# TensorE's idle products removed from a two-block transformer kernel on one core

## Time and profile before

| | |
|---|---|
| median of three runs | 2423.07 us |
| the profiled execution | 2424.09 us, its span 2422.3 us |
| busy in the span: TensorE products | 2374.6 us (98%) |
| TensorE weight loads | 2012.1 us (83%) |
| VectorE | 1622.1 us (67%) |
| ScalarE | 1115.2 us (46%) |
| GpSimd | 461.2 us (19%) |
| mean granted TensorE clock | 0.995 |
| DMA | 264.29 MB, mean 109 GB/s |

### The profile page before, as it was taken

One profiled execution on the slowest core, in us unless ns is written; L12 is line 12 of the kernel. 1 busy time (PEld: TensorE's weight loads), 2 busy tenths in 40 slices (PEclk: granted clock), 3 DMA queues, 4 the chain that ended last, 5 costly groups with the idle time before them and its releaser, 6 DMA issues.

```text
span 2422.3 us, 38419 instructions
## 1 busy us (share of the span) xinstructions
PE 2374.6 (98%) x16018; PEld 2012.1 (83%) x16018; DVE 1622.1 (67%) x2296; ACT 1115.2 (46%) x1671; POOL 461.2 (19%) x183
## 2 busy tenths in 40 slices
PE   8998989999999999999999999999999999999999
PEld 7747875798989888889898989999887778888887
DVE  6578867896867765679675697666616636666514
ACT  6663544362525445545353554332425435555533
POOL 1312203100000102410000002333134333111234
PEclk9999998999999999999999999999999999999999
DMA  7222453335354343224332323222222322121121
GB/s 298 87 92 66 79 126 139 115 112 185 109 195 158 129 148 114 97 95 149 116 113 94 114 101 122 70 75 83 79 87 89 108 89 103 70 70 70 62 89 67
DMA packets 94413, 264.29 MB, mean 109 GB/s; under 512 B 55201, under 2 KB 55841, under 8 KB 69281
## 3 DMA queue, kind: packets, MB, share of 16 engines
q1 hardware_dynamic: 91936, 253.46, 30.3%
q10 hardware_dynamic: 2304, 8.39, 1.0%
HBM read 256.05 MB, written 5.78 MB: 108 GB/s over the span
## 4 chain that ended last, share of the span: by engine, by line
PE 83%; DVE 8%; issue 3%; DMA 3%; ACT 2%; SPq 0%; DVEq 0%; ACTq 0%; POOL 0%; POOLq 0%
PE bank L357 15%; PE bank L359 15%; PE bank L358 14%; PE bank L2608 6%; PE bank L2610 6%; PE bank L2611 6%; PE bank L290 2%; PE bank L288 2%; PE bank L289 2%; PE bank L4773 1%; DMA ring<-in_stream 1%; PE bank L270 1%; DMA ada_slot<-in_first 1%; PE bank L266 1%; PE bank L267 1%
## 5 line engine op out<-in xcount | busy, mean ns | idle before, releaser
L388 POOL TENSOR_TENSOR ring_low<-ring,w_high 128x2048 fp32r<-128x2048 f32 (+1 forms) x79 | 355.1, 4496 | 1614.3 <-ACT w_high L378 1614.3
L378 ACT ACTIVATE w_high<-ring 128x2048 fp32r<-128x2048 f32 (+1 forms) x128 | 234.7, 1839 | 221.9 <-PE bank L359 212.2
L357 PE MATMUL bank<-h_high,w_high 128*128 128x512 f32 (+1 forms) x480 | 192.3, 401 | 0.0
L359 PE MATMUL bank<-h_high,ring_low 128*128 128x512 f32 (+1 forms) x480 | 190.3, 396 | 0.0
L358 PE MATMUL bank<-h_low,w_high 128*128 128x512 f32 (+1 forms) x480 | 189.1, 394 | 0.0
L357 PE MATMUL bank<-z_high,w_high 128*128 128x512 f32 x380 | 151.3, 398 | 0.1
L359 PE MATMUL bank<-z_high,ring_low 128*128 128x512 f32 x380 | 150.4, 396 | 0.0
L358 PE MATMUL bank<-z_low,w_high 128*128 128x512 f32 x380 | 149.6, 394 | 0.0
L2611 PE MATMUL bank<-h_high,ring_low 128*128 128x256 f32 x528 | 147.2, 279 | 0.0
L359 PE MATMUL bank<-hidden_high,ring_low 128*128 128x512 f32 x352 | 139.5, 396 | 0.0
L357 PE MATMUL bank<-hidden_high,w_high 128*128 128x512 f32 x352 | 139.5, 396 | 0.0
(11 more groups left out here) (594 smaller groups left out, 6802.0 us busy)
## 6 DMA issues: line engine op xcount, KB each, us to landing
ring<-in_stream SPq DMA_DIRECT2D x186, 1024.0 KB, 4.8
ada_slot<-in_ada_next SPq DMA_DIRECT2D x40, 512.0 KB, 4.4
ada_slot<-in_gains SPq DMA_DIRECT2D x17, 512.0 KB, 4.3
ada_slot<-in_first SPq DMA_DIRECT2D x16, 512.0 KB, 4.3
scale_weights<-in_first SPq DMA_DIRECT2D x4, 1024.0 KB, 23.4
inverse<-scratch_inverse SPq DMA_DIRECT2D x32, 128.0 KB, 3.3
x_res<-in_x SPq DMA_DIRECT2D x2, 1024.0 KB, 8.6
w_first<-in_first SPq DMA_DIRECT2D x2, 1024.0 KB, 16.3
```

The source lines that it names most:

```text
L357: pe.matmul(out, w_high[:, k, cols], x_high, start=start, stop=False)
L359: return pe.matmul(out, w_low[:, k, cols], x_high, start=False, stop=stop)
L378: act.activation(self.high_buf[:, b % 2, 0:cols], self.c.ring[:, b % SLOTS, 0:cols], ACT.Copy)\
L388: pool.tensor_tensor(self.c.ring_low[:, b % SLOTS, 0:cols], self.c.ring[:, b % SLOTS, 0:cols], self.high_buf[:, b % 2, 0:cols].bitcast(F32 ...
```

## The change

All calls of `keep_warm` are taken out, and the function with them: 79 products, 158 instructions. No wait, no buffer and no other instruction is changed.

```
@@ Tail.tensor (three borders)
             pe.matmul(c.bank[4][:, j:j + 1], self.acc[:, tok(j)], c.ones[:, 0:1], start=(j == 0), stop=False)
-        c.keep_warm(pe, 1)
         pe.wait_ge(self.squared.sem, self.squared.of(KD - 1))
...
         mm.then_inc(self.mean.sem, 1)
-        c.keep_warm(pe, 2)
         pe.wait_ge(self.inverse.sem, self.inverse.of(0))
...
         mm.then_inc(self.spread.sem, 1)
-        c.keep_warm(pe, 8)
@@ first stage, tensor
         pe.wait_ge(squared.sem, squared.of(0))
-        chip.keep_warm(pe, 16)
         pe.wait_ge(total_of.sem, total_of.of(KD - 2))
...
         mm.then_inc(mean.sem, 1)
-        chip.keep_warm(pe, 4)
         pe.wait_ge(inverse.sem, inverse.of(0))
...
         shift_block(0)
-        chip.keep_warm(pe, 6)
         shift_block(1)
@@ rwkv_output, tensor
         mm.then_inc(var_mm.sem, 1)
-        chip.keep_warm(pe, 12, 0)
...
         for n in range(4):
             spread_tile(n)
-        chip.keep_warm(pe, 8, 0)
```

More of the change, by code:

```diff
@@ L197, in take_groups @@
         return u
-    def keep_warm(self, pe, n, bank=7):
-        for _ in range(n):
-            pe.matmul(self.bank[bank][:, 0:P], self.ident[:, :], self.ones[:, :], start=True, stop=True)
     def slot(self, b, kt):
```

## The result

Median of five runs 2436.45 us (2431.78 to 2440.89), against 2422.66 us (2420.98 to 2424.65) of the kernel before, measured beside it: ratio 1.0054, 95% interval [1.0037, 1.0070]. The changed kernel is slower by 13.1 us in the means (13.8 in the medians); the forecast was 6.4. The profiled execution took 2436.45 us, its span 2434.6 us, mean granted clock 0.987 in place of 0.995.

The account below looks back on a forecast made before the run. TensorE, busy 98% of the span, was taken to set the time. Start +2.1, group norm +2.1 and borders +2.2 gave +6.4 us: median 2423.1 to 2429.5, range 2427.0 to 2432.5, wider 2425.0 to 2435.0.

Parts of the forecast that it names:

- the term of the start: Start: products meet the low clock and L942 ends later; +2.1 us left after slack, bounds +0.7 and +3.9.
- The term of the borders: Three borders: a clock fall at half the visits, 1.5 us each; +2.2 us, bounds -0.2 and +9.2.
- The clock as the cause: All five places: without idle products TensorE's clock is low, 1.2 in place of 2.4 GHz; +6.4 us in all.
- The start's own delay: Start: VectorE's L1208 waits 2.8 us longer for L942; +2.1 us left after slack up to block b_r.
- Spacing and record: Start: product spacing and recorded clock disagree, spacing decides; by record -0.3 us, by spacing +2.1.
- check (4): Between the changed places: equal times for equal work; a difference would make the prediction wrong even with its total right.
- The group norm: Group norm: a certain clock fall slows the output projection, +1.5 us, and the spread, +0.6; sum +2.1, bounds +0.7 and +3.2.
- A fall at every second visit: Three borders: the clock falls at half the visits, 1.5 us a fall; 3 x 0.5 x 1.5 = +2.2 us.
- 263.9 to 267.3: Stretch of the trace before, TensorE busy 1.60 of 3.4 us without a following clock fall; compared with the borders.
- the first rival: Only start and group norm lose the clock, no border falls: 2427.1 us, 0.17% slower; chance 27%.
- Every border falls and comes back late: Rival at the three borders: +9.2 us there, 2436.5 us in all; chance 12%.
- The long low spell: Last rival, recurrence: 13.7 us at half clock cost up to 6.4 us, independent of the change; within the remaining 3%.

Follow-up runs that it names:

- one_column: Kernel before with all 79 idle products kept but each moving one column in place of 128: 2437.10 us, ratio 1.0057.
- no_start_period: Kernel before without the start's 26 idle products, with 64 tiny products ahead of TensorE's first wait: 2430.38 us, ratio 1.0030.
- the tiny products: Kernel before without the start's 26 idle products, with 26 one-column products ahead of TensorE's first wait: 2424.97 us, ratio 1.0013.
- no_gn: Kernel before with only the group norm's idle products (12 and 8) taken out: 2425.19 us, ratio 1.0010.
- no_border: Kernel before with only the borders' idle products (1, 2 and 8, three times) taken out: 2427.69 us, ratio 1.0014.

## Why the prediction was wrong

The direction, the clock's part and the group norm were right; the cost of the start and of the borders was not, and the range ended below the measured time. The step that failed is the term of the start, +2.1 us for all that its removal costs: it measured 7.3. The term of the borders, +2.2, measured 3.4.

- **The clock as the cause: right, for all but some 5 us.** The changed kernel's clock is low at all five places, and so is one_column's, with the same occupation and one column. That one_column's total agrees as well is partly luck (above).
- **The start's own delay: right.** +2.1 us at block b_r was forecast and read, though its parts differ: VectorE got the shift 2.5 us late, not 2.8, because the clock rose at 21.9, not 23.2 us, while the chain began 0.35 us later. Spacing and record don't disagree, as the prediction had it: the trace's first entry of the granted clock stands at 14.71 us in before and at 21.94 in after, just where the spacing changes, and the 1.00 that the view shows ahead of it (from 10 to 12 us in after too, with nothing running) is no record.
- **"The start: I take +2.1" as the whole cost of removing it: wrong, and the largest error.** It measured 7.3 us (7.9 in no_start_period), of which 2.0 to 2.9 are the clock's. The rest, 4.5 to 5.1 us, comes from the 104 instructions as instructions, as the tiny products show. That it comes by the fetches of TensorE's code, moved onto small transfers of the recurrence, is shown for one transfer and 1.8 us, and argued for the rest. The prediction's own check (4), "equal times for equal work" between the places, was where it failed. The trace of before could have shown it: the page's queue list has q8, the issues have block_rows, but I priced removed instructions by their busy time alone.
- **The group norm: right,** +2.1 forecast, +2.0 in the profile, +2.1 in no_gn's means. The parts are right too: +0.4 on the spread's chain (+0.6 forecast) and +1.6 in the projection (+1.5).
- **"A fall at every second visit" of a border "and 1.5 us a fall": wrong in both factors.** All nine visits without idle products that were profiled fell, at 1.9 to 3.4 us. In cost against the kernel before it is less far off, +3.4 us in place of +2.2, because that kernel falls at borders as well; the profile of before hid this. The comparison that left it open was a poor one. That the clock didn't fall behind 263.9 to 267.3 was chance: at the same work it fell in 8 of the 14 profiles. In no_border, which is the kernel before up to there (its busy times by stretch):

```profile
263.90:267.30 3.40, 1.06 (x21) 0.82 (x17) 3.06 (x14) 2.29 (x7) 0.00 (x0) 1.00 0.72 155
267.30:270.70 3.40, 3.40 (x60) 3.28 (x62) 3.19 (x7) 0.60 (x1) 0.00 (x0) 0.50 0.78 286
```

It was also a comparison by busy time (and the busier of the two stretches, 1.86 us, was the one that fell), while one_column shows that busy time isn't what counts, and L580 and L584 fill 2 us of a border with 16 columns in all. By the Trainium skill (TensorE: Matmul & The Clock Gate, "Loop structure matters more than you think") a long idle wait before the products lets the clock drop. At the borders it dropped without one: at the second border of the changed kernel it was low from 830.9 us, ahead of the spread and of the wait of 1.69 us, behind waits of 0.25 and 0.34 us and products of one column. So the first rival, that no border falls, is refuted.
- **The rival that came out at 2436.5: luck.** "Every border falls and comes back late" is within 0.1 us of the measured median, and every border did fall. But it put 9.2 us on the borders (3 x 3.1 is 9.3), which cost 3.4 in the means (7.5 in the two profiles), and had nothing for the 5 us that the moved instructions cost.
- **The long low spell: as said.** The last rival's 13.7 us at half clock in before were 3.4 in the changed kernel, which took 4.8 us off its profile; how often either kernel has it in its other runs no profile tells.
- **The range: too narrow from two omissions.** Three runs of before, 3.7 us apart, gave no idea of its real spread of 13 us, and the bounds of the sum had no term for what moves when code shrinks.

## What to carry to other kernels

Here an idle product of 128 columns held the clock through a stretch that had little else, and one of a single column did not, at the same place and with the same weight loads. So look at the columns between two dense stretches, not at busy time. Removing or adding TensorE instructions also moves its code fetches against everything behind them, so a control that restores the number of instructions (tiny ones where the engine idles anyway) belongs to each experiment of a few microseconds. And where the clock falls by chance, one profile of either kernel can flatter it by as much as the effect: here by up to about 4 us at the borders (7.5 in two profiles, 3.4 in the means), and by 4 to 6 us the other way in the recurrence.

## What the runs showed of the hardware

- The code of TensorE comes by DMA in packets of 16 KB, 125 to 127 of them here, about 256 instructions apart. One such packet took 0.9 to 1.9 us; a 64 KB transfer of 64-byte packets met by one landed after 4.0 to 4.4 us in place of 2.4 to 3.0.
- TensorE's clock rose at 14.7 us behind idle products from 9.9 on, at 21.9 us (no idle products) behind full-width work from 18.7 on, and at 23.0 us in one_column, where products of one column had followed each other since 9.59 and full-width ones since 19.82.
- At the second border of after it fell at 830.9 us; since the last full-width product there had been waits of 0.25 and 0.34 us and about ten instructions of one column.
- At the low level plain float32 instructions of 128 columns follow each other at 0.213 us in place of 0.112, and those of one column too.
- Ninety executions of the same kernel took 2417.8 to 2430.7 us, and at the same work, near 267 us, the clock fell in 8 of 14 profiles.
